# A float32 transformer kernel: the SBUF addresses of its weight units and activation rows are moved to multiples of 2 KB

## The reference, cut to what matters

```python
x = x + merged @ w_out                      # first block: RG-LRU branch + pooling branch, gated
x = x + (gelu(up[:, :F]) * up[:, F:]) @ w_down   # up = conv(rms_norm(x) @ w_up), F = 2816
h = x + gate1 * ((sig(ga)*y_ssm + sig(gb)*y_att) @ w_out_2)   # second block: S5 scan + sparse attention
h = h + gate2 * ((silu(u2 @ w_gate) * (u2 @ w_up_2)) @ w_down_2)
return rms_norm(h, final_g)
```

## The kernel before, in words

| tensor | address | mod 2048 | mod 256 |
|---|---|---|---|
| raw | 16,512 | 128 | 128 |
| whi | 32,896 | 128 | 128 |
| wlo | 49,280 | 128 | 128 |
| vec | 65,664 | 128 | 128 |
| cst | 67,616 | 32 | 32 |
| sml | 69,152 | 1568 | 32 |
| rows of tiles, 76 | 73,408 | 1728 | 192 |

## Time and profile before

### The profile page before, as it was taken

How to read it: one execution, slowest core, us unless ns; L and a number is a source line. 1 busy time by engine, 2 the same in 40 slices (tenths; PEclk the granted TensorE clock), 3 DMA queues, 4 the chain that set the end, 5 groups by cost and what they waited for, 6 DMA issues and landing times.

```text
span 1527.4 us, 18719 instructions
## 1 busy us (share of the span) xinstructions
PE 1492.1 (98%) x7256; PEld 1207.9 (79%) x7256; DVE 732.5 (48%) x1373; ACT 854.1 (56%) x1099; POOL 248.8 (16%) x275
## 2 busy tenths in 40 slices
PE   9999999999999999999997999999999999999998
PEld 7877888887878888888876777876878888888886
DVE  5788643555596958443134457925663212110011
ACT  6778876935565546554443575488345444444441
POOL 1111111111111111111112431121011111111111
PEclk9999999999999999999998999999999999999999
DMA  9777887799999798799879867986587998888882
GB/s 263 186 172 169 198 181 187 184 304 304 294 252 272 206 223 218 186 272 232 212 200 290 242 154 187 211 249 216 153 205 186 236 233 194 192 190 196 188 184 83
DMA packets 98648, 324.71 MB, mean 213 GB/s; under 512 B 10992, under 2 KB 13040, under 8 KB 98432
## 3 DMA queue, kind: packets, MB, share of 16 engines
q0 software_dynamic: 34400, 125.17, 44.2%
q1 hardware_dynamic: 60624, 191.39, 37.1%
q10 hardware_dynamic: 3536, 6.95, 1.2%
HBM read 179.69 MB, written 18.87 MB: 130 GB/s over the span
## 4 chain that ended last, share of the span: by engine, by line
PE 80%; DMA 8%; DVE 6%; ACT 4%; issue 1%; SPq 1%; POOL 0%; ACTq 0%; DVEq 0%
PE ps L687 25%; PE ps L688 25%; PE ps L690 24%; DMA wlo<-raw 3%; DMA raw<-in_w 2%; DVE pl_f L1914 1%; DMA pl_f<-stk 1%; ACT whi L1117 1%; ACT wlo L1126 1%; DMA tab<-pl_f 1%; PE ps L731 1%; DVE pl_r L1527 1%; PE ps L1011 1%; PE ps L1031 1%; DMA pl_f<-tab 1%
## 5 line engine op out<-in xcount | busy, mean ns | idle before, releaser
L687 PE MATMUL ps<-pl_r,whi 128*128 128x512 f32 x1976 | 783.3, 396 | 10.7 <-DMA wlo<-raw 5.6
L688 PE MATMUL ps<-pl_r,wlo 128*128 128x512 f32 x1976 | 775.3, 392 | 0.0
L690 PE MATMUL ps<-pl_r,whi 128*128 128x512 f32 x1976 | 774.2, 392 | 0.0
L687 PEld LDWEIGHTS ps<-pl_r,whi 128*128 128x128 f32 x1976 | 372.5, 189 | 101.9 <-issue 15.2
L690 PEld LDWEIGHTS ps<-pl_r,whi 128*128 128x128 f32 x1976 | 372.0, 188 | 84.7 <-DVE pl_r L1544 0.9
L688 PEld LDWEIGHTS ps<-pl_r,wlo 128*128 128x128 f32 x1976 | 372.6, 189 | 78.0 <-issue 0.5
L2259 POOL DMA_DIRECT2D wlo<-raw x238 | 203.8, 858 | 1173.2 <-ACT wlo L1126 1145.7
L1117 ACT ACTIVATE whi<-raw 128x1024 fp32r<-128x1024 f32 x247 | 259.9, 1053 | 184.8 <-PE ps L690 132.5
L1126 ACT ACTIVATE wlo<-raw 128x1024 fp32r<-128x1024 f32 x238 | 248.8, 1045 | 0.0
L1527 DVE TENSOR_TENSOR pl_r<-pl_f,pl_r 128x512 fp32r<-128x512 f32 x116 | 80.3, 692 | 44.7 <-ACT pl_r L1146 28.3
L2231 DVE TENSOR_TENSOR pl_f<-ps,pl_f 128x512 f32<-128x512 f32 x22 | 15.2, 691 | 172.9 <-PE ps L690 172.9
(11 more groups left out here) (263 smaller groups left out, 1089.4 us busy)
## 6 DMA issues: line engine op xcount, KB each, us to landing
raw<-in_w SPq DMA_DIRECT2D x245, 512.0 KB, 5.3
wlo<-raw POOLq DMA_DIRECT2D x238, 512.0 KB, 6.2
pl_f<-in_mod SPq DMA_DIRECT2D x48, 512.0 KB, 9.5
pl_f<-tab SPq DMA_DIRECT2D x12, 512.0 KB, 8.0
xs<-pl_f SPq DMA_DIRECT2D x16, 256.0 KB, 7.2
tab<-pl_f SPq DMA_DIRECT2D x8, 512.0 KB, 5.8
pl_f<-xs SPq DMA_DIRECT2D x16, 256.0 KB, 5.2
spill<-pl_f ACTq DMA_DIRECT2D x16, 256.0 KB, 4.8
```

The costliest lines, as they stand in the source:

```text
L687: matmul(out, wh, sr(pair, kk, "hi"), start=start, stop=False)
L688: matmul(out, wl, sr(pair, kk, "hi"), start=False, stop=False)
L690: mm = matmul(out, wh, sr(pair, kk, "lo"), start=False, stop=stop)
```

## The change

The order in which tensors are allocated changes. `vec` and `cst` stand in front, then 80 columns named `lamr` as a tensor of their own (`lams`, taken out of `sml`), then a gap of 160 bytes, then `raw`, `whi`, `wlo`, the 76 rows of tiles, and behind them what is left of `sml` (981 columns). The number of rows was computed from what was left of SBUF, and came to 76; it is now the constant 76.

```diff
+NSLOT = 76
@@ SMALL
-         ("need", 1), ("nm", 16), ("rsm", 16), ("lamr", 80), ("lami", 80), ("ckr", 64), ("cki", 64),
+         ("need", 1), ("nm", 16), ("rsm", 16), ("lami", 80), ("ckr", 64), ("cki", 64),
@@ Kit.__init__
+        row = 4 * S
+        self.vec = sb("vec", [128, NV])
+        self.cst = sb("cst", [128, 3, 128])
+        self.lams = sb("lams", [128, 80])
+        self.ident, self.ones, self.tri = (self.cst[:, i, :] for i in range(3))
+        start = (nc.sbuf_base + 31) // 32 * 32
+        sb("gap", [128, -start % row // 4])
         self.raw = sb("raw", [128, NRAW, UB * 128])
         self.whi = sb("whi", [128, NHI, UB * 128], F32R)
         self.wlo = sb("wlo", [128, NLO, UB * 128], F32R)
-        self.vec = sb("vec", [128, NV])
-        self.cst = sb("cst", [128, 3, 128])
+        self.base = (nc.sbuf_base + 31) // 32 * 32
+        assert self.base % row == 0
+        self.slots = NSLOT
+        sb("slots", [128, NSLOT * S])
         self.sml = sb("sml", [128, NSML])
-        self.ident, self.ones, self.tri = (self.cst[:, i, :] for i in range(3))
-        self.base = (nc.sbuf_base + 31) // 32 * 32
-        self.slots = (nc.sbuf_usable_end - self.base) // (4 * S)
@@ sm
+        if name == "lamr":
+            return self.lams[:, j:j + n]
         return self.sml[:, SOFF[name] + j:SOFF[name] + j + n]
```

## The result

| | before | after |
|---|---|---|
| median of the runs, us | 1526.40 (5 runs, 1524.48 to 1530.94) | 1518.66 (5 runs, 1517.00 to 1519.40) |
| ratio, 95% interval | | 0.9942 [0.9924, 0.9960] |
| span of the profiled execution | 1527.4 | 1518.1 |

The kernel became faster by 0.6%. The time lies in the range that was forecast (1516 to 1534), but not where the likeliest case had it (1525.5, with 1521 to 1531 around it): there was an effect, and it is in the step of the matmuls. By the prediction's own border of 0.5% this is, just, its case "faster", to which it gave 0.15, and not "same", to which it gave 0.75. The two profiled executions lie 9.3 us apart and the two medians 7.7, since the one of before was slower than its median by more than the one of after; what follows is read from the profiled ones.

The account below looks back on a forecast made before the run. It took TensorE's float32r step to bound the kernel; with DMA at -0.5 us and other terms 0, 1528.67 became 1528.2, less 2.7 us for the profiled execution's excess over the median: 1525.5 us, range 1516 to 1534.

Parts of the forecast that it names:

- likeliest case: Whole kernel: no effect that shows, chance 0.65, with a median of 1525.5 us.
- The bound: TensorE: 5928 float32r matmuls at a step of 0.2290 us make 1357.5 us, 89% of the span.
- VectorE, ScalarE, plain float32: Operand starts on VectorE, ScalarE and in plain float32 matmuls on TensorE: moving them was valued at 0 each.
- DMA: Transfers of raw, additions and rows: value -0.5 us, bounds -4 to +4 us.
- float32r at 0: TensorE's float32r matmuls: new operand starts leave the step unchanged, value 0, with -93 and +93 us kept as rivals.
- Rival A: float32r moving rows: aligned rows save a 128-byte piece, step 215.7 ns, 79 us less, 1447 us; chance 0.14 in full or part.
- Rival B: float32r row reads and weight loads collide in equal phase: 23 us slower, 1549 us; chance 0.09 including other PE step losses.

Follow-up runs that it names:

- the one line: The kernel before with only the base of the 76 rows moved by 192 bytes, from 73,408 to 73,600: 1518.52 us, ratio 0.9951 to the kernel before.
- e1: The kernel after with the 76 rows back at 1728 past a multiple of 2048 and the units at 0: 1546.47 us, ratio 1.0107 to the kernel before.

## Why the prediction was right or wrong

**The bound.** Right: PE's step of float32r, paid 5928 times, is what the time follows. The six kernels are in order of their step: 226.7 ns has ratios 0.9942, 0.9935 and 0.9951, 229.0 has 1, 232.4 has 1.0086, and 233.3 has 1.0107.

**VectorE, ScalarE, plain float32.** Right, each at 0: busy times within 1 us, 429.1 to 429.2 ns at all three starts. The evidence that the prediction had for plain float32, equal durations, was weaker than it was taken to be: an end is modelled, and only starts show a step.

**DMA.** Right in that it gives the kernel nothing: the runs with everything at 64 and with the one line, where raw again starts off a 256-byte boundary, have the whole gain, and the landings went from 5.3 and 6.2 us to 5.4 and 6.3. The prediction weighed the rule of the Trainium skill ("DMA: Bandwidth & Descriptors", How a descriptor splits into AXI transactions), by which, as an estimate, both queues should have lost some 3% of their time. They didn't, but q0, which carries the additions, shows a part of it. It went from 44.2% of 1527.4 us to 43.8% of 1518.1, 1.5% less. Of its 30,496 packets of 4096 bytes, 26,226 took 326 to 330 ns in the kernel after and 26,085 in the one with only the units aligned; in the four kernels with units at 64 or 128 past such a boundary it was 16,056 to 17,676, and some 9,100 to 10,100 took 334 to 360 ns, against 1,100 in the first two. So where the units start does something to these packets, of up to about the size of the rule, and where the rows start does nothing that shows. q1, which brings the units in, went from 37.1% to 37.5%, 0.5% more, and its 4096-byte packets have a median of 159 ns in all six kernels: there nothing of the rule is seen.

**float32r at 0.** This is the step that failed: a term put at nothing, which measured 2.3 ns a matmul. I wrote that the row nearest to this case, L688 from 394 to 397 ns over all rows and weight positions, "shows no sign of an address". It could not: within a layout every distance from row to weight block is a multiple of 512 bytes plus a constant, and the effect has a period of 256. A row that never varies the quantity says nothing on it. The prediction said itself "For a finer shift there is only a bound", and took 0 all the same. It also read one line of three: in the trace of before the three lines have 392, 394 and 388 ns at one shape, a difference that asked for an explanation and is gone in the kernel after. The value should have been -13.6 us, of which 9.3 came through between the profiled executions. The prediction's own mark for being wrong, a change of the step by 1.3 ns, was passed with 2.3. That the time still fell into 1516 to 1534 is luck: that range had been widened for small parts of A and B, whose mechanisms are not what acted, and the effect happened to be small.

**Rival A** (rows off a 128-byte line touch 17 pieces) forecast the right sign and six times the size (79 us against 13.6), and its mechanism is refuted: rows at 64 or 1728 with weights at the same have 226.9 ns, and rows at 128, which are on such a line, have 232.4 with weights at 0. That 17/16 gave 229 was a coincidence. The 16-byte lines of the Trainium skill ("SBUF — State Buffer", Door 1: The DMA port swizzle), which spoke against A, don't explain a difference between 0 and 64 either.

**Rival B** (equal phase makes the two reads meet) had the right pair of reads and the wrong sign: of the distances tried at 512 columns and 128 weight columns, equal phase is the best. What spoke against B, plain float32 in equal phase, was no evidence on float32r in either direction: it doesn't react to any of the three distances that were tried (0, 4 and 64).

**Where a third of the gain went.** The step alone is worth 13.6 us; 4.1 us came back as idle time of PE, named above, and that explains most of the gap to 9.3. The layouts on the slow side show the same: e1's step costs 5928 x 4.3 ns = 25.5 us, its span grew by 17.9, and PE's idle time fell from 35.3 to 1545.3 - 1513.7 = 31.6 us.

The rest can be found from the starts of all 7256 matmuls. Idle time leaves out the first part of every wait, since a matmul is drawn 0.39 us long where the next could start after 0.23. Of the distances from one start to the next, 5878 lie between two float32r matmuls and 1377 elsewhere. From before to after the first save 5878 x 2.2 = 12.9 us by the step (228.9 to 226.7) and take 3.1 us more in waits above the step, and the others take 0.9 more: 8.9 us less in all. From before to e1 it is 5878 x 4.4 = 25.9 us more by the step, 4.6 us less in waits, and 3.3 less elsewhere: 18.0 us more. So both sums close to within half a microsecond of the spans: a change of the step is paid back in part by waits for work that keeps its own pace.

**Open.** What the two reads share, why the period is 256, and what makes 240.0 ns of distance 120 were not found; the runs show the dependence and not its cause.

## What to carry to other kernels

When a float32r kernel is bound by TensorE and works with 512 moving columns and 128 weight columns, try the moving rows and the weight blocks at the same start mod 256, and then look at the step from start to start in a stretch without gaps; it is a change of one line. With other shapes measure the distances first: with 256 columns distance 0 was the slowest, with 384 it made no difference against 64, and with 96 or 64 weight columns another distance was better. Aligning one side alone can cost: here it was 0.9% and 1.1%. And when a row of the trace is taken as evidence that something doesn't matter, ask first whether the thing varies in it.

## What the runs showed of the hardware that was not expected

- A float32r matmul of 512 columns (128 weight columns) steps in 226.7 to 240.0 ns with nothing else running, by the distance between its two operands in SBUF; for starts at multiples of 64 the distance mod 256 gives the step, as long as all matmuls of the sequence have the same one. bfloat16 (215.8, five distances) and plain float32 (429.1 to 429.2 a pass, three) showed no dependence.
- At distance 0 the surplus over a column a cycle is 13.3 ns for 512, 384 and 256 columns alike. At other distances it depends on the shape: at 64 it is 15.6 ns for 512 columns, 13.4 for 384 and 11.1 for 256, and with 256 columns it can be 10.7 (117.3 ns).
- At distance 0, with fewer weight columns the step of a 512-column float32r matmul is longer and not shorter: 226.7 ns with 128, 230.0 with 96 and with 64, 231.6 with 32.
- DMAs that add one SBUF tensor onto another had half as many again of their packets near 328 ns with both tensors at a multiple of 256 bytes (26,226 of 30,496) as with both at 128 past one (17,676), and this made the kernel no faster.
